# The value sum of a product-key expert layer with its matmul operands exchanged

## What is computed

```python
u = expert_u[idc]
a = jax.nn.gelu(jnp.einsum('cd,ckd->ck', xc, u))
vv = expert_v[idc]
return jnp.einsum('ck,ckd->cd', gc * a, vv)
...
x = x + peer(h2, peer_w_q[l], peer_sub_keys[l], peer_u[l], peer_v[l])
return rmsnorm(x, final_norm_g)
```

## Time and profile before

| | |
|---|---|
| median of 3 runs | 2281.08 us |
| lowest and highest | 2278.61 and 2281.27 us |
| span of the profiled execution, first to last instruction | 2281.8 us |
| mean granted clock of TensorE | 0.968 of full speed |
| PE matmul busy, share of the span | 2144.9 us, 94% |
| DVE, ACT, POOL busy | 64%, 35%, 37% |
| first matmul of the value stage starts | 1554.66 us |
| chain's matmul part ends, last DVE instruction ends | 2271.86, 2278.74 us |

### The profile page before, as it was taken

How to read it: one execution, slowest core, us unless ns; L and a number is a source line. 1 busy time by engine, 2 the same in 40 slices (tenths; PEclk the granted TensorE clock), 3 DMA queues, 4 the chain that set the end, 5 groups by cost and what they waited for, 6 DMA issues and landing times.

```text
span 2281.8 us, 33765 instructions
## 1 busy us (share of the span) xinstructions
PE 2144.9 (94%) x10616; PEld 1744.1 (76%) x10616; DVE 1463.3 (64%) x3578; ACT 793.8 (35%) x1136; POOL 850.5 (37%) x361
## 2 busy tenths in 40 slices
PE   6988999999999999888888888899999999999998
PEld 5766788887888888667777777788888888888886
DVE  6687212213179997999999999604555555555555
ACT  5566423224222223333433433322222222222223
POOL 4311244443345444222222222244444444444442
PEclk9999999999999999998998999999999999999999
DMA  5211122222234444345434544475555555456442
GB/s 203 83 38 38 47 93 100 92 92 74 83 121 142 141 148 138 89 164 170 126 117 166 170 156 124 147 259 188 192 196 181 181 204 183 175 179 219 176 175 102
DMA packets 108517, 323.48 MB, mean 142 GB/s; under 512 B 11200, under 2 KB 11200, under 8 KB 106304
## 3 DMA queue, kind: packets, MB, share of 16 engines
q1 hardware_dynamic: 108192, 322.49, 42.0%
q10 hardware_dynamic: 288, 0.54, 0.1%
HBM read 253.78 MB, written 69.21 MB: 142 GB/s over the span
## 4 chain that ended last, share of the span: by engine, by line
PE 46%; issue 32%; DVE 13%; POOL 8%; DVEq 0%; POOLq 0%
PE bank L635 31%; PE bank L438 14%; DVE ohI L1325 9%; POOL w_lo L415 8%; DVE ohJ L1323 3%; PE bank L718 1%; DVEq L1325 0%; DVE x_sb L1369 0%; POOLq L414 0%; DVEq L1323 0%; POOLq L418 0%; PE bank L703 0%; DVE x_sb L1364 0%; POOL mask L399 0%; POOL mask L401 0%
## 5 line engine op out<-in xcount | busy, mean ns | idle before, releaser
L415 POOL TENSOR_TENSOR w_lo<-raw,w_hi 128x1024 fp32r<-128x1024 f32 x346 | 846.8, 2448 | 1412.2 <-ACT w_hi L760 1412.2
L760 ACT ACTIVATE w_hi<-raw 128x1024 fp32r<-128x1024 f32 x346 | 366.8, 1060 | 1300.9 <-PE bank L438 761.5
L438 PE MATMUL bank<-hT_hi,w_hi 128*128 128x512 f32 x1488 | 605.8, 407 | 0.5 <-POOL w_lo L415 0.4
L438 PE MATMUL bank<-hT_lo,w_hi 128*128 128x512 f32 x1488 | 592.7, 398 | 0.0
L438 PE MATMUL bank<-hT_hi,w_lo 128*128 128x512 f32 x1488 | 592.2, 398 | 0.0
L1347 DVE TENSOR_TENSOR wT_lo<-wf,wT_hi 128x512 fp32r<-128x512 f32 x128 | 314.9, 2460 | 132.0 <-ACT wT_hi L991 132.0
L1325 DVE TENSOR_SCALAR ohI<-iota_b,IT,R 128x128 bf16<-128x128 bf16 x1024 | 338.1, 370 | 0.0
L438 PEld LDWEIGHTS bank<-hT_hi,w_hi 128*128 128x128 f32 x1488 | 288.8, 194 | 62.3 <-issue 3.8
L438 PEld LDWEIGHTS bank<-hT_hi,w_lo 128*128 128x128 f32 x1488 | 287.3, 193 | 63.0
L438 PEld LDWEIGHTS bank<-hT_lo,w_hi 128*128 128x128 f32 x1488 | 288.5, 194 | 58.8 <-issue 0.7
L635 PE MATMUL bank<-w_hi,wT_hi 128*128 128x512 f32 x1024 | 321.4, 396 | 0.0
(11 more groups left out here) (216 smaller groups left out, 1488.9 us busy)
## 6 DMA issues: line engine op xcount, KB each, us to landing
raw<-stream SPq DMA_DIRECT2D x346, 512.0 KB, 3.5
a_rows<-abuf SPq DMA_DIRECT2D x128, 256.0 KB, 4.0
g_rows<-gstage SPq DMA_DIRECT2D x32, 1024.0 KB, 6.1
g_in<-g_rows SPq DMA_DIRECT2D x16, 2048.0 KB, 8.9
a_in<-a_rows SPq DMA_DIRECT2D x128, 256.0 KB, 3.5
x_sb<-x SPq DMA_DIRECT2D x4, 512.0 KB, 8.7
out<-x_sb SPq DMA_DIRECT2D x4, 512.0 KB, 2.7
subkeys<-subkeys SPq DMA_DIRECT2D x1, 1024.0 KB, 14.2
```

Source lines behind the costliest of these rows:

```text
L415: pool.tensor_tensor(w_lo[:, k % 2, :], raw[:, k % RAW, :], w_hi[:, k % 2, :].bitcast(f32), ALU.subtract).then_inc(lo_ready, 1)
L438: last = pe.matmul(dst, w[:, slot, k * P:(k + 1) * P], rhs[low][:, r0 + k - k0, :], start=(k == k0 and wi == 0), stop=(k == k1 - 1 and wi ...
L760: act.activation(w_hi[:, base % 2, :], raw[:, slot, :], ACT.Copy).then_inc(hi_ready, 1)
```

## The change

In the value stage the operands of each matmul change places. A 128x128 piece k of the chunk (128 experts x 128 output channels) is stationary, and the weighted activations of all 512 tokens move past it into bank k. The sum comes out turned: bank k holds output channels k of all tokens. The number of matmuls, their passes and their width stay (8 x 3 = 24 a chunk). At the end each bank is copied to a new buffer `yF`, banks 0, 2, 4, 6 by DVE and 1, 3, 5, 7 by ACT, 32 transposes on PE turn it back in two halves of 16, and DVE adds the result to `x_sb` as before, but all four tiles of the left half first and then those of the right half. `yF` lies over the gates' buffer `g_in`, slot 0.

```diff
+        yF = Place(late + 2 * T * 4 * 2)("yF", [KC, T])
...
+                wT = (wT_hi, wT_lo)
                 chunk(n + i0)
                 pe.wait_ge(weighted_lo, i0 + (di + 1))
-                spread_sum(n % 2, (wT_hi[:, di % 2, :], wT_lo[:, di % 2, :]), first, final,
-                           before=a_read if first else None, order=(1, 2, 3, 0) if first else range(TT))
+                for k in (2, 3, 4, 5, 6, 7, 0, 1) if first else range(KC):
+                    if first and k == 0:
+                        pe.wait_ge(proj_read, R_U + NI)
+                    for wi, (w, low) in enumerate(passes):
+                        last = pe.matmul(bank[k][:, :], w[:, n % 2, k * P:(k + 1) * P], wT[low][:, di % 2, :],
+                                         start=first and wi == 0, stop=final and wi == 2)
+                    if final and k < KC - 1:
+                        last.then_inc(summed, 1)
+                last.then_inc(chunk_used, 1)
...
+            for half in range(2):
+                pe.wait_ge(y_out_dve, 2 * half + 2)
+                pe.wait_ge(y_out_act, 2 * half + 2)
+                for t in range(TT):
+                    for k in range(4):
+                        last = pe.transpose(bank[4 * half + t][:, k * P:(k + 1) * P],
+                                            yF[:, 4 * half + k, t * P:(t + 1) * P], ident[:, :])
+                    last.then_inc(y_turned, 1)
...
+            for k in range(1, KC, 2):
+                if k < KC - 1:
+                    act.wait_ge(summed, TT - 1 + k + 1)
+                else:
+                    act.wait_ge(chunk_used, CHUNKS)
+                act.activation(yF[:, k, :], bank[k][:, :], ACT.Copy).then_inc(y_out_act, 1)
...
+            for k in range(0, KC, 2):
+                dve.wait_ge(summed, TT - 1 + k + 1)
+                dve.tensor_copy(yF[:, k, :], bank[k][:, :]).then_inc(y_out_dve, 1)
             dve.wait_ge(gfin_loaded, 16)
-            for t in range(TT):
-                if t < TT - 1:
-                    dve.wait_ge(summed, TT - 1 + t + 1)
-                else:
-                    dve.wait_ge(chunk_used, CHUNKS)
-                for half in range(2):
-                    cols = slice(half * 512, (half + 1) * 512)
-                    last = dve.tensor_tensor(x_sb[:, t, cols], x_sb[:, t, cols], bank[2 * t + half][:, :], ALU.add)
-                last.then_inc(x3_ready, 1)
+            for half in range(2):
+                cols = slice(half * 512, (half + 1) * 512)
+                for t in range(TT):
+                    dve.wait_ge(y_turned, 4 * half + t + 1)
+                    last = dve.tensor_tensor(x_sb[:, t, cols], x_sb[:, t, cols], bank[4 * half + t][:, :], ALU.add)
+                    if half:
+                        last.then_inc(x3_ready, 1)
```

More of the change, by code:

```diff
@@ L235, in build @@
         summed = sem("summed")
+        y_out_dve, y_out_act, y_turned = sem("y_out_dve"), sem("y_out_act"), sem("y_turned")
         gfin_loaded = sem("gfin_loaded")
@@ L725, in _ @@
             pe.wait_ge(gate_read, 2 * I_GATES + 2)
-            def a_read(t):
-                if t == 0:
-                    pe.wait_ge(proj_read, R_U + NI)
             def weigh(i0, di, first=False, final=False):
                 n = S_EV + di
+                wT = (wT_hi, wT_lo)
                 chunk(n + i0)
                 pe.wait_ge(weighted_lo, i0 + (di + 1))
-                spread_sum(n % 2, (wT_hi[:, di % 2, :], wT_lo[:, di % 2, :]), first, final,
-                           before=a_read if first else None, order=(1, 2, 3, 0) if first else range(TT))
+                for k in (2, 3, 4, 5, 6, 7, 0, 1) if first else range(KC):
[7 more added lines that the diff above has]
+                last.then_inc(chunk_used, 1)
             for i in range(2):
```

## The result

| | before | changed |
|---|---|---|
| median of 9 runs | 2279.98 us | 2286.36 us |
| lowest and highest | 2277.83, 2283.09 us | 2285.47, 2289.49 us |
| ratio, with its 95% interval | | 1.0026 (1.0018 to 1.0035) |
| span of the profiled execution | 2281.8 us | 2287.7 us |
| mean granted clock | 0.968 | 0.968 |

The changed kernel is 6.4 us slower by the medians, 4.1 to 8.0 us by the interval. The forecast was +8.1 us and 2289.2, so its difference lies just above that interval.

What follows compares the result with a forecast made beforehand. PE was taken to bound the value stage through matmul count and spacing. Turned matmuls +2.5 us and the longer end +5.6 us gave +8.1 us, 2281.1 to 2289.2 us; range 2284.5 to 2293.

Steps and rivals of the forecast that it cites:

- That PE bounds the stage, and that only the distance counts there: Value stage: time is the number of matmuls times the spacing of their starts, 233.4 ns before, plus what follows the last.
- Part 1: Turned matmuls of the value stage: spacing goes from 233.4 to 234.2 ns over 3,071 distances, +2.5 us.
- the third kind: Matmuls with a chunk's piece stationary and `yT` moving, 234.2 ns apart in the trace before.
- Rival B: Value stage: the two buffers together set the pace whatever their roles, so it stays 233.4 ns; 2286.7 us, chance 0.18.
- An operand there, on either side, costs the 7 ns: Operands 32 bytes past a multiple of 64 from the arena's start, or further back, slow a matmul, stationary or moving.
- Rival A: Value stage: the moving operand's place doesn't matter for `wT`, so matmuls run at 226.8 ns; 2266.4 us, chance 0.08.
- Part 2: End behind the last value matmul: copies, transposes, adds, first root and scalings make it 5.6 us longer, bounds 4.7 and 7.7.
- T0: End of the last matmul of the value stage, 2271.86 us in the profile before.
- 8 x 0.68 us: DVE's eight adds at the end, 0.68 us each, setting the pace: done at T0 + 5.97.
- 1 us for starting code not run before: Allowance in the upper bound of the end's growth, beside +1.1 us for slow transposes; that bound was 7.7 us.
- Rival C: End: PE slips to half clock during transposes, 0.85 us per four, so DVE waits; 2290.3 us, chance 0.13.
- Back-to-back issue gap: Skill section giving matmul spacing by moving columns alone, 512/2.4 + 2.5 = 216 ns; by it the change of roles is free.

Runs made afterwards that it cites:

- after_front32: Changed kernel with everything behind the small tensors (`yT`, `mg`, `wT` among them) moved by 32 bytes: 2270.35 us, 0.9954 of the kernel before.
- before_all0: Kernel before with 608 and 896 unused bytes, so `memT`, `yT`, `mg` and `wT` begin at multiples of 2,048 bytes from `w`: 2256.64 us, 0.9892 of before.
- before_wT0: Kernel before with 480 unused bytes ahead of `wf`, so `wT` begins at a multiple of 512 bytes from `w`: 2261.24 us, 0.9920 of before.
- after_wT0: Changed kernel with 480 unused bytes ahead of `wf`, so `wT` begins at a multiple of 512 bytes from `w`: 2266.64 us, 0.9945 of the kernel before.
- before_hT32: Kernel before with `hT_hi` and `hT_lo` alone moved by 32 bytes against `w`: 2298.37 us in one run.
- after_all32: Changed kernel with the whole arena's contents moved by 32 bytes: 2287.83 us in one run.
- before_front32: Kernel before with everything behind the small tensors moved by 32 bytes: 2280.93 us, 0.9998 of the unmoved kernel before.
- after_wT256: Changed kernel with 224 unused bytes ahead of `wf`, so `wT` begins 256 bytes past a multiple of 512 from `w`: 2268.87 us in one run.
- after_front64: Changed kernel with everything behind the small tensors moved by 64 bytes: 2286.38 us in one run.
- after_wT128: Changed kernel with 96 unused bytes ahead of `wf`, so `wT` begins 128 bytes past a multiple of 512 from `w`: 2285.16 us in one run.

## Why the prediction was right, and where it was not

- **That PE bounds the stage, and that only the distance counts there**: right. Same waits, no idle PE, and where the distance changed, the time followed: after_front32, both versions with `wT` at 0 and before_all0, each timed four times or more, came out faster by about what their distances give.
- **Part 1, 234.2 ns, +2.5 us**: wrong by its whole size; measured 0. The failed step is "after the change the pair is a chunk's piece against `wT`, which is the third kind". I sorted matmuls by whether a buffer lay off a multiple of 64 bytes, and `yT` and `wT` are both 32 past one. What counts is the distance to the other operand within 256 bytes: 160 for `yT`, 32 for `wT`. Rival B, pace unchanged because the two buffers together set it, named the right reason and gave 2286.7 us, within 0.4 us of the measured 2286.36.
- **"An operand there, on either side, costs the 7 ns"**: the 7 ns are real, the place is not. before_wT0 and after_wT0 take them off, before_hT32 puts them on, after_all32 shows that the place alone does nothing.
- **Rival A** (226.8 ns) was a property of the layout, not of the order: 480 bytes bring it about in either order. As the layout stood, it could not happen.
- **Part 2, the end, +5.6 us**: measured +5.2. The mechanism was right step by step: no add before T0, first add at T0 + 0.54 (forecast 0.55), copies hidden, the first root held up by the table load. The size was off in one term, "8 x 0.68 us": an add costs 0.60 us from start to start, not 0.68. I divided the merged row of eight adds by eight, but it includes DVE's pauses while PE finished the next tile; the two copies in the earlier trace rows, 0.61 apart, would have shown it. That makes the fifth add end 0.3 us earlier; the rest of the 0.4 is rounding on the way to "T0 + 7.0", for 3.95 + 2.76 + 0.2 are 6.9. The "1 us for starting code not run before" in the upper bound stood on no row, and the trace shows no such time: the first transpose starts at 2272.37, 0.23 us behind the start of the last matmul.
- **Rival C** (slow transposes): did not happen; 109 ns and clock 1.00 behind steady matmuls. The page TensorE: Matmul & The Clock Gate of the Trainium skill says in its section PE-mode transpose that the full clock does not engage for transposes. The trace doesn't agree over this length: 32 in a row, 3.50 us, kept 1.00.
- **Back-to-back issue gap**: this section of the same page of the Trainium skill gives 216 ns by the columns alone, as the prediction says, but for an isolated matmul. For a stream in which each matmul has a weight load it says that both set the spacing, and gives about 131 ns at 512 columns; the prediction left that out. The runs agree with neither figure: at 512 columns and full clock they show 226.7, 229, 233.3 and 234.2 ns, by the operands' distance. That the change of roles costs the stream nothing came true all the same.
- **The total**: +8.1 forecast, +6.4 measured. The forecast less the 2.5 and 0.4 us above is the 5.2 us that the traces show at the end, and the interval of the medians' difference, 4.1 to 8.0, holds that. The side came out right by Part 2. That the total came out close although the theory of Part 1 was wrong is luck of the size: the theory chose between values 0.8 ns apart here, and the same theory missed by some 24 us where another layout put it to the test (before_front32, expected near 2256).

## What to carry over

Exchanging stationary and moving operand, with number and width of matmuls kept, changed nothing in the stream at the distances of 32 and 0 bytes; at 64 bytes it gained 4 ns a matmul. Where the pace stays, what decides is what the turned result needs afterwards: here no token is complete before the last matmul, and adds that ran beside matmuls now stand behind them. Before one explains a few per cent between matmuls of equal shape by their roles, banks or inputs, one should look at where the operands start relative to each other; here some padding was worth 1.1%, more than the change cost. And a merged row of back-to-back instructions may hide pauses: its mean isn't the price of one.

## What was not expected of the hardware

The distance between the starts of the two operands, taken within 256 bytes, sets the pace of 128x128 by 128x512 matmuls with a weight load each, at full clock:

| distance of the second buffer from `w` | moving | stationary |
|---|---|---|
| 0 | 226.7 ns (`wT`, `yT`), 226.8 ns (`hT`) | 226.7 ns (`wT`, `mg`) |
| 32 | 233.3 ns (`wT`, `hT`) | 233.3 ns (`wT`) |
| 64 | 229 ns (`wT`) | 233.3 ns (`wT`) |
| 96, 128 | 233.3 ns (`wT`) | not tried |
| 160 | 234.2 ns (`yT`) | 233.4 ns (`mg`) |
| 192 | 233.3 ns (`yT`) | 233.3 ns (`mg`) |
| 224 | 233.3 ns (`yT`) | 233.3 ns (`mg`) |

These are means over adjacent starts of one stream without its few longer gaps, hence 226.7 and 233.3 where whole stretches above gave 226.8 and 233.4. The row of 0 is from after_wT0, after_wT256, before_wT0 and before_all0 (`hT` from before), that of 32 from before, after and before_hT32, 64 and 192 from the two shifts by 32, 96 and 224 from after_front64, 128 from after_wT128, 160 from before.

Shifting both by 32 bytes changes nothing. Why it is so isn't shown. The next piece's weight load runs beside the current matmul; in the changed kernel:

```profile
2262.10 0.39 PE L738 MATMUL bank<-wT_lo,w_hi 128*128 128x512 f32 x1
2262.11 0.19 PEld L738 LDWEIGHTS bank<-wT_hi,w_lo 128*128 128x128 f32 x1
```

So a piece of one buffer is read while the other streams, and reads that get in each other's way at some distances would fit; no run here looks at it directly. Why `wT` at 64 bytes is faster as the moving operand only is open too; there the two kernels differ also in their loops and banks.
